# Strassen's seven products on half of K in seven FFN blocks of a two-layer fp32 trunk on Trainium2, with the weight sums made by adding DMAs

## Reference

```python
D_FF = 5632
for i in range(2):
    mod = silu(c) @ ada_w[i] + ada_b[i]        # six vectors of 2048
    ...                                        # mixer, residual, LayerNorm
    h = x * (1.0 + sc_f) + sh_f                # 256 x 2048
    y = (silu(h @ ffn_w1[i]) * (h @ ffn_w3[i])) @ ffn_w2[i]
    x = layer_norm(alpha * x + (1.0 + g_f) * y, ...)
```

## Time and profile before

| what | us |
|---|---|
| median of 3 runs (2192.49 to 2194.15) | 2193.56 |
| the profiled execution, given by its span | 2191.0 |
| PE busy in it | 2139.0 (98%) |
| DVE busy | 1596.9 (73%) |
| ACT busy | 990.1 (45%) |
| mean granted TensorE clock | 0.998 of full |
| DMA moved | 635.90 MB, mean 290 GB/s |

### The profile page before, as it was taken

The page is one execution under the profiler, slowest core; times in us unless marked ns, Lnnn a source line. Parts: engine busy times, 40 slices in busy tenths (PEclk is TensorE's granted clock), DMA queues, the critical chain, the costliest instruction groups (busy, mean ns, idle before and its releaser), DMA issues.

```text
span 2191.0 us, 24820 instructions
## 1 busy us (share of the span) xinstructions
PE 2139.0 (98%) x9557; PEld 1744.3 (80%) x9557; DVE 1596.9 (73%) x1792; ACT 990.1 (45%) x1291; POOL 105.1 (5%) x208
## 2 busy tenths in 40 slices
PE   5799999999999999999999999999999999999999
PEld 2378887888888888888788888878888888888887
DVE  6789999777777777778877666878775555455566
ACT  1077646444443444443544455554444433444443
POOL 2101100000000000000000000000000000000000
PEclk9999999999999999999999999999999999999999
DMA  9999997889998898999589788958987765666773
GB/s 387 418 364 362 363 388 285 276 292 341 337 340 319 320 340 322 318 350 361 193 287 331 264 273 282 338 175 290 332 295 226 234 194 191 214 212 213 219 239 124
DMA packets 177064, 635.90 MB, mean 290 GB/s; under 512 B 20385, under 2 KB 51377, under 8 KB 150705
## 3 DMA queue, kind: packets, MB, share of 16 engines
q1 hardware_dynamic: 147298, 427.93, 56.0%
q0 software_dynamic: 27792, 201.34, 24.6%
q10 hardware_dynamic: 1856, 5.04, 0.6%
HBM read 616.37 MB, written 17.86 MB: 289 GB/s over the span
## 4 chain that ended last, share of the span: by engine, by line
PE 86%; DMA 6%; DVE 6%; ACT 2%; issue 1%; POOL 0%; ACTq 0%; SPq 0%; DVEq 0%; POOLq 0%
PE ps L1862 53%; PE ps L1868 27%; PE ps L1879 3%; DMA gate<-in_ada_w 3%; DMA raw<-in_mla_w_o 1%; DVE wlo L1167 1%; DMA ada_head<-in_ada_w 1%; DVE ada_w L1204 1%; DVE gate L1204 1%; DMA ada_w<-in_ada_w 1%; DMA raw<-in_mla_w_uv 1%; PE ps L2091 0%; ACT whi L710 0%; DVE ada_head L1204 0%; PE ps L2121 0%
## 5 line engine op out<-in xcount | busy, mean ns | idle before, releaser
L1167 DVE TENSOR_TENSOR wlo<-raw,whi 128x1024 fp32r<-128x1024 f32 (+1 forms) x717 | 867.1, 1216 | 513.8 <-ACT whi L710 512.7
L710 ACT ACTIVATE whi<-raw 128x1024 fp32r<-128x1024 f32 (+1 forms) x717 | 756.1, 1056 | 1033.8 <-PE ps L1868 952.4
L1862 PE MATMUL ps<-whi,hT_hi 128*128 128x512 f32 x1880 | 585.7, 393 | 1.5 <-DVE hT_lo L1595 1.5
L1862 PE MATMUL ps<-whi,hT_lo 128*128 128x512 f32 x1880 | 579.5, 389 | 0.0
L1868 PE MATMUL ps<-wlo,hT_hi 128*128 128x512 f32 x1880 | 502.7, 389 | 0.0
L1862 PEld LDWEIGHTS ps<-whi,hT_lo 128*128 128x128 f32 x1880 | 352.9, 188 | 74.0
L1868 PEld LDWEIGHTS ps<-wlo,hT_hi 128*128 128x128 f32 x1880 | 352.9, 188 | 73.7
L1862 PEld LDWEIGHTS ps<-whi,hT_hi 128*128 128x128 f32 x1880 | 350.1, 188 | 72.9 <-DVE hT_lo L1595 2.0
L1204 DVE CUSTOM_DVE_ANT_0 ada_w<-ada_w,c_bc,cols 128x2048 f32<-128x2048 f32 x145 | 339.8, 2345 | 16.4 <-ACT c_bc L1050 8.4
L1862 PE MATMUL ps<-whi,uT_hi 128*128 128x512 f32 x656 | 202.0, 389 | 0.0
L1862 PE MATMUL ps<-whi,uT_lo 128*128 128x512 f32 x656 | 201.9, 389 | 0.0
(11 more groups left out here) (274 smaller groups left out, 1470.0 us busy)
## 6 DMA issues: line engine op xcount, KB each, us to landing
raw<-in_ffn_w SPq DMA_DIRECT2D x528, 512.0 KB, 4.7
ada_w<-in_ada_w POOLq DMA_DIRECT2D x145, 1024.0 KB, 7.6
raw<-in_fox_w_in SPq DMA_DIRECT2D x96, 512.0 KB, 5.3
ada_head<-in_ada_w POOLq DMA_DIRECT2D x16, 1024.0 KB, 20.3
raw<-in_mla_w_o SPq DMA_DIRECT2D x32, 512.0 KB, 8.6
raw<-in_fox_w_o SPq DMA_DIRECT2D x32, 512.0 KB, 5.5
gate<-in_ada_w POOLq DMA_DIRECT2D x12, 1024.0 KB, 9.0
ada_low<-in_ada_w POOLq DMA_DIRECT2D x10, 1024.0 KB, 10.4
```

The lines of the kernel that those rows point to most:

```text
L710: nc.scalar.activation(split_hi(pl.unit)[:, 0:n], raw[:, s, 0:n], ACT.Copy).then_inc(hi_ready, 1)
L1167: nc.vector.tensor_tensor(split_lo(pl.unit)[:, 0:n], raw[:, s, 0:n], split_hi(pl.unit)[:, 0:n].bitcast(F32), ALU.subtract).then_inc(lo_rea ...
L1862: nc.tensor.matmul(ps[:, 2 * pair + t, 0:width], a[:, t * P:(t + 1) * P], w_hi, start=(first and c == 0 and a is hi), stop=False)
```

## The change

In blocks 4 to 10 of layer 1's FFN (FAST_FROM = 4; seven blocks) the first half of K, four units deep, is done in two groups (MIXES = 2) by the Winograd form of Strassen's algorithm. The 2 x 2 blocks of the left matrix are row half t by K unit x of the group; those of the right are K unit by (w1, w3). Each of the seven products is an operand of 6 matmuls (operand), 128 rows by 512 columns into one bank. Four of them take as stationary a sum of h blocks (S1 to S4), made once on DVE while block 3 runs (mix_inputs, mix_low) and split by ACT (mix_high) into tiles that lie where c_bc and ada_w were; DVE's modulation work is therefore finished earlier (one product after every second unit in the first half of block 3, and no spare ones at the end of block 2). The weight sums T1 to T4 are not computed by an engine: POOL issues a DMA with accumulate onto the raw slot that still holds the previous operand, after its lo has been made. Their chain in a slot is B11, T1, T2, T4, and B22, T3 in another. The other half of K is done in plain units of 12 matmuls. A block has thus 22 units in the ring in place of 16, in the order of FAST_UNITS, in which group 1 follows group 0 at seven operands' distance.

Raw slots are 7 (two more lie where c_bc was, over the mixing's own input, so that loads into them wait for mix_ready), given out by raw_slots(), and a load waits for the lo of the last unit in its slot. The banks are: 0 to 3 the products of B11, T1, T2 and T3; 4 and 5 w1's plain half with B21 and T4; 6 and 7 w3's plain half with B22. DVE and ACT combine them (fast_block on each), into silu_all and u. PE waits for both pairs before each fast block, for mix_ready before the first, for each bank's reader in the fast block before, and after each pass for all of them. Units are counted from the block's start below: 0 is B11 of group 0, 21 the last plain unit.

```diff
+FAST_FROM = 4
+MIXES = 2
+FAST_GROUPS = range(MIXES)
+PLAIN_UNITS = range(2 * MIXES, PAIRS)
+FAST_BLOCKS = range(FAST_FROM, sum(FF_PASSES))
+S1, S2, S3, S4 = range(4)
+W1, W3 = "ffn_w1", "ffn_w3"
+def fast_units():
+    w1 = iter([("plain", j, W1, j, None) for j in PLAIN_UNITS])
+    w3 = iter([("plain", j, W3, j, None) for j in PLAIN_UNITS])
+    part = {"B11": (W1, 0, None), "B21": (W1, 1, None), "B22": (W3, 1, None), "T1": (W3, 0, "B11"),
+            "T3": (W3, 0, "B22"), "T2": (W3, 1, "T1"), "T4": (W1, 1, "T2")}
+    def mix(kind, g):
+        name, which, onto = part[kind]
+        return kind, g, name, 2 * g + which, onto
+    return [mix("B11", 0), mix("B21", 0), mix("B22", 0), next(w1), next(w1), mix("T1", 0), mix("T3", 0),
+            mix("B11", 1), mix("B21", 1), mix("B22", 1), next(w1), next(w1),
+            mix("T2", 0), mix("T1", 1), mix("T3", 1), next(w3), mix("T4", 0), mix("T2", 1),
+            next(w3), next(w3), mix("T4", 1), next(w3)]
...
+    for n, kind in enumerate(UNIT_KINDS):
+        if n < FAST_START:
+            s = n % RING
+        elif kind and kind[4]:
+            s = held.pop((kind[4], kind[1]))
+        else:
+            s = min((m for m in range(RAWS) if m not in held.values()), key=lambda m: last[m])
+        if kind and any(u[4] == kind[0] for u in FAST_UNITS):
+            held[kind[0], kind[1]] = s
+        slots.append(s)
+        before.append(last[s] + 1)
+        last[s] = n
...
+                if RAW_FREE[n]:
+                    sp.wait_ge(lo_ready, RAW_FREE[n])
+                if RAW_SLOT[n] >= RING:
+                    sp.wait_ge(mix_ready, 1)
+                sp.dma_start(raw_of(n)[:, 0:source.shape[-1]], source).then_inc(raw_in[RAW_SLOT[n]], 16)
...
+            def load_fast(first, i):
+                for n, (kind, g, name, j, onto) in enumerate(FAST_UNITS):
+                    if onto:
+                        pl.unit += 1
+                        continue
+                    load(A[name][1, i * PAIRS + j])
+                    if i > first and n == U_OUT_AFTER:
+                        u_out(1, i - 1)
+                    if i > first and n == U_BACK_AFTER:
+                        u_back(1, i - 1)
...
+                            pool.wait_ge(lo_ready, RAW_FREE[n])
+                            pool.dma_start(raw_of(n), A[name][1, i * PAIRS + j], accum_op=ALU.add
+                                           ).then_inc(sum_in[kind == "T3"][g], 16)
...
+            def fast_block(n, i):
+                b = i - FAST_FROM
+                units(AT["B11"] + 4)
+                act.wait_ge(units_used, pl.pe - 4)
+                act.wait_ge(u_flipped, U_BLOCKS + i)
+                nc.scalar.activation(silu_all[:, 0, :], ps[:, 0, :], ACT.Copy).then_inc(first_copied, 1)
+                units(AT["T1"] - AT["B11"] - 4)
+                act.wait_ge(units_used, pl.pe)
+                nc.scalar.activation(u[:, 1, :], ps[:, 1, :], ACT.Copy).then_inc(fifth_copied, 1)
+                units(AT["T3"] - AT["T1"])
+                if i > sum(FF_PASSES[:n]):
+                    u_high(1, n, i - 1)
+                units(AT["T4"] + 1 - AT["T3"])
+                act.wait_ge(left_done, b + 1)
+                nc.scalar.activation(silu_all[:, :, :], silu_all[:, :, :], ACT.Silu).then_inc(fast_silu, 1)
+                units(FAST_COUNT - AT["T4"] - 1)
...
+                        if l == 1 and first + i == FAST_FROM - 1:
+                            units(MIX_AT)
+                            act.wait_ge(mix_summed, 1)
+                            nc.scalar.activation(s_hi[:, :, :, :], s_32[:, :, :, :], ACT.Copy).then_inc(mix_high, 1)
+                            units(PAIRS - MIX_AT)
...
+            def mix_inputs():
+                assert pl.ada == len(ADA_ORDER), pl.ada
+                dve.wait_ge(ada_done, pl.ada)
+                chunks = 2 * UC * MIXES
+                chain(nc.vector.tensor_tensor(mix32[:, :, :], hT_hi[:, 0:chunks, :].bitcast(F32),
+                                              hT_lo[:, 0:chunks, :].bitcast(F32), ALU.add))
+                of = mix32[:, :, :].rearrange("p (g x c) (t n) -> p x t g c n", x=2, c=UC, t=T)
+                out = s_32[:, :, :, :].rearrange("p s (g c) n -> p s g c n", c=UC)
+                (a11, a21), (a12, a22) = ([of[:, x, t] for t in range(T)] for x in range(2))
+                s = [out[:, n] for n in range(4)]
+                mark(nc.vector.tensor_tensor(s[S1], a21, a22, ALU.subtract))
+                mark(nc.vector.tensor_tensor(s[S3], a11, a21, ALU.subtract))
+                own()
+                chain(nc.vector.tensor_tensor(s[S2], s[S1], a11, ALU.subtract))
+                nc.vector.tensor_tensor(s[S4], s[S2], a12, ALU.add).then_inc(mix_summed, 1)
+            def mix_low():
+                dve.wait_ge(mix_high, 1)
+                nc.vector.tensor_tensor(s_lo[:, :, :, :], s_32[:, :, :, :], s_hi[:, :, :, :].bitcast(F32),
+                                        ALU.subtract).then_inc(mix_ready, 1)
+            def fast_block(n, i):
+                b = i - FAST_FROM
+                units(AT["T3"])
+                if i > sum(FF_PASSES[:n]):
+                    u_low(1, n, i - 1)
+                units(AT["T2"] - AT["T3"])
+                dve.wait_ge(units_used, pl.pe)
+                dve.wait_ge(first_copied, b + 1)
+                chain(nc.vector.tensor_tensor(u[:, 0, :], silu_all[:, 0, :], ps[:, 2, :], ALU.add))
+                nc.vector.tensor_tensor(silu_all[:, 1, :], u[:, 0, :], ps[:, 3, :], ALU.add).then_inc(sixth_read, 1)
+                units(1)
+                dve.wait_ge(fifth_copied, b + 1)
+                dve.wait_ge(sixth_read, b + 1)
+                chain(nc.vector.tensor_tensor(u[:, 0, :], u[:, 1, :], u[:, 0, :], ALU.subtract))
+                mark(nc.vector.tensor_tensor(u[:, 1, :], u[:, 1, :], silu_all[:, 1, :], ALU.subtract))
+                units(AT["T4"] - AT["T2"] - 1)
+                dve.wait_ge(units_used, pl.pe)
+                own()
+                nc.vector.tensor_tensor(silu_all[:, :, :], silu_all[:, :, :], ps[:, 4:6, :], ALU.add
+                                        ).then_inc(left_done, 1)
+                units(FAST_COUNT - AT["T4"])
+                dve.wait_ge(units_used, pl.pe)
+                nc.vector.tensor_tensor(u[:, :, :], u[:, :, :], ps[:, 6:8, :], ALU.add).then_inc(right_read, 1)
+                dve.wait_ge(right_read, b + 1)
+                dve.wait_ge(fast_silu, b + 1)
+                chain(nc.vector.tensor_tensor(u[:, :, :], silu_all[:, :, :], u[:, :, :], ALU.mult))
+                flip(1, i, u)
...
+                        elif l == 1 and first + i == FAST_FROM - 1:
+                            units(1)
+                            mix_inputs()
+                            units(MIX_AT)
+                            mix_low()
+                            units(PAIRS - 1 - MIX_AT)
                         else:
-                            units_with_ada(PAIRS, 2)
+                            units_with_ada(PAIRS, 0 if (l, i) == (1, FAST_FROM - 2) else 2)
...
+            def operand(bank, stationary, first, end):
+                s = pl.unit % RING
+                pe.wait_ge(hi_ready, pl.unit + 1)
+                for c, (hi, lo) in enumerate(stationary):
+                    for a in (hi, lo):
+                        nc.tensor.matmul(ps[:, bank, :], a, whi[:, s, c * NB:(c + 1) * NB],
+                                         start=(first and c == 0 and a is hi), stop=False)
+                pe.wait_ge(lo_ready, pl.unit + 1)
+                for c, (hi, lo) in enumerate(stationary):
+                    ins = nc.tensor.matmul(ps[:, bank, :], hi, wlo[:, s, c * NB:(c + 1) * NB],
+                                           start=False, stop=(end and c == UC - 1))
+                ins.then_inc(units_used, 1)
+                pl.unit += 1
...
+            def fast_block(i):
+                b = i - FAST_FROM
+                pair_free(pl.block)
+                pair_free(pl.block + 1)
+                if b == 0:
+                    pe.wait_ge(mix_ready, 1)
+                for kind, j, name, _, _ in FAST_UNITS:
+                    first, end = j == 0, j == MIXES - 1
+                    if kind == "B11":
+                        if b and first:
+                            pe.wait_ge(first_copied, b)
+                        operand(0, rows_of_h(j, 0, 0), first, end)
+                    if kind == "T1":
+                        if b and first:
+                            pe.wait_ge(fifth_copied, b)
+                        operand(1, mixed(S1, j), first, end)
+                    if kind == "T2":
+                        if b and first:
+                            pe.wait_ge(sixth_read, b)
+                        operand(2, mixed(S2, j), first, end)
+                    if kind == "T3":
+                        if b and first:
+                            pe.wait_ge(sixth_read, b)
+                        operand(3, mixed(S3, j), first, end)
```

(87 more changed lines are left out.)

77 lines of the change are left out of this document (60 added, 17 removed).

## The result

The changed kernel takes 2300.26 us (2297.48 to 2301.8) against 2193.41: a ratio of 1.0484, interval 1.0469 to 1.0499, 107 us slower. The forecast was 2215 with a range of 2185 to 2248: the direction was right, the size wrong by a factor of five (107 us for 21.3). The page of the kernel after: span; busy by engine; shares of the chain by engine and by line.

What follows compares the result with a forecast made beforehand. The prediction took TensorE (PE), busy 98% of 2191.0 us, as the bound. Its terms, -19.0 + 8.0 + 3.9 + 7.7 + 5.5 + 11 + 4.2, summed to +21.3, so 2215 us, with a range of 2185 to 2248.

Steps and rivals of the forecast that it cites:

- The saving: In seven fast blocks, 84 matmuls fewer at 0.2267 us each: -19.0 us.
- the four boundaries: PE waits at the entries of blocks 4 (8.0 us) and 6 (3.9) and the exits after 5 and 10 (7.7).
- the five joints: Between fast blocks, B22 waits for banks 6 and 7, free at 3.8 but needed at 2.72: 5.5 us in all.
- The entry of block 4: First loads wait for the mixed inputs, so PE starts at 27.0 in place of 19.0: 8.0 us (bounds 3.9 and 11).
- the term of the adding DMAs: In six blocks with u's traffic, T4 of group 1 comes 1.8 us late: 11 us (bounds 0 and 35).
- L: Duration of one 512 KB adding DMA, taken as 6.5 us, between 5.4 and 7.8.
- The load of unit 11: Queued behind u's eight returns, goes at 13.4 us into the block, lands at 18.8, split just in time: no wait.
- The bound of 6.8: Load time in us behind the adding DMAs' upper bound of 35 us, with additions at 7.8.
- a rival with a chance of 0.14: DMA rings become the bound, an addition taking its engines as long as two loads: 2265 us, milder forms 2240 to 2270.
- The clock: After long PE waits the clock falls, once at block 4's entry and half a fall elsewhere: 4.2 us (0 to 11).
- Sums in time (1): Rival: adding DMAs land like loads, under 5.6 us: 2200 to 2204 us, still slower; chance 0.18.
- Faster (3): Rival: at boundaries and joints banks come free when PE asks, DVE's evictions not behind splits: 2180 us; chance 0.22.

Runs made afterwards that it cites:

- e4: The change with u's DMAs later in SP's queue and the sums' operands as independent plain SP loads, weight additions left out: 2210.77 us.
- e1: The change with u stored behind the load of unit 11 and read back behind that of unit 15 (was 9 and 10): 2271.18 us.
- e10: The change with e1's edit and POOL's DMAs copying instead of adding (weight additions left out), in the change's own order: 2236.87 us.
- e5: The change with the edits of e1 and e3, both groups in step in another order of units, u split later: 2226.86 us, ratio 1.0155.
- e3: The change with DVE reading banks before the splits ahead of them, products' banks swapped in pairs, PE waiting for a pair only where written: 2275.71 us.
- e7: The change with filler matmuls on PE, 20 before each of five joints' waits and 38 before each of two exits' waits: 2299.2 us.
- e6: The change with the edits of e3 and e4 together (weight additions left out): 2179.46 us, ratio 0.9933 to the kernel before.
- e11: e5 with one group in place of two, and the mixing's input moved off the two added raw slots: 2186.04 us, ratio 0.9966.

## Why the prediction was wrong

**Right.** The saving (84 matmuls), PE as the bound before, the four boundaries and the five joints as places of new waits. e4, where only they are left, shows their sum within 1 us of the forecast: 26.1 us for 25.1 (10.0 + 8.0 + 4.4 + 3.7). The entry of block 4 was 2.0 low, the joints 1.1 high in all.

**The step that failed** is the term of the adding DMAs, 11 us with bounds of 0 and 35, measured at 60 (e1 less e4), and at 89 with the load behind u's returns (the change less e4). Taken away one after the other, the loss of 107 us is 29 for the place of u's DMAs (change to e1), 34 for the adding (e1 to e10), 26 for the chain of DMAs and POOL's queue (e10 to e4) and 17 for the boundaries less the saving (e4 to before); in another order the parts differ. Four things in the term:

1. "Whatever the duration L, T4 is ready at 26.6 + 2L, so the wait begins at L = 5.6." This asked when PE needs the sum. But T4's split is in DVE's program ahead of the reads that free six of the eight banks (2 and 3 by L1845 and L1846, 4 and 5 by L1855, 6 and 7 by L1859; ACT reads 0 and 1). Once its lead is short, each microsecond lost moves those reads, before PE waits for the sum. e10 shows it: with copies PE waits 0.3 us for a sum, and joints, exits and the entry still take 18.5 us more. By an estimate on the forecast's own clock, DVE needs 9.5 us from T4's split to the left-half addition and 1.2 for that, and PE gets from T4 to B21 in 5.4, so T4 had to be ready 5.3 us before PE wants it, at 32.5 in place of 37.8; with 26.6 + 2L that is L = 3.0, less than even the quiet load's 3.9. In the change T4 came only when PE asked, so the joints took 4.6 us each in place of 1.1, for the left half that the forecast had at 0 with 0.3 to spare, and the exits 8.7 in place of 3.9.
2. The load of unit 11 was to go 13.4 us into the block and land 5.4 later, "just in time", as in the stage at 330 GB/s. In block 7 it went at 19.4 and took 9.0, with adding DMAs on the same rings: u was stored at 10.9, where the forecast had it flipped at 6.4, late because the joint itself waits 4.65 us, and the eight returns took 5.4 to issue for 3.75. So the late read feeds the late load, and that the next sums. The bound of 6.8 was no bound. e1 prices it at 29 us; the place was right, the size was not.
3. L was taken as 6.5; the median is 7.9 (7.1 in the added slots), at the upper bound of 7.8. In the forecast's own formula this gives 4.6 us in place of 1.8 in six blocks, 28 for 11: the size of L alone is the smaller part of the miss.
4. What an addition does to the others was left to a rival with a chance of 0.14. It holds the rings 2.8 to 3.0 us, twice a load. In the change's own order the rings still had gaps (0.86 in a block), so this came in as latency; in e5 it is the bound itself. That rival's price, 2240 to 2270, was low for the change (2300), and it had the joints at 1.1 too; e5, where the rings are the bound and e3's edits have taken most of the boundaries, is under it at 2227.

**The clock** was given 4.2 us. Matmuls took 39 us longer in the change, but e7 shows that this is no term of its own there: taking away some 23 us at the lower level bought nothing, since the chain sets the pace. In e4, where no chain does, PE is busy 8.4 us longer for it, twice the forecast and inside its 0 to 11.

**The rivals.** Sums in time (1) had 2200 to 2204; e4 without any chain has 2211, by the entry and the clock above, and e10, whose chain of copies lands near that rival's 5.6, has 2237, by the step that failed. Faster (3) needed DVE's reads ahead of their splits: e3 and e6 made that, and e6's 2179 is where that rival put it (2180), but only with no chain. The change itself leaves the splits first, as the forecast said against this rival.

## What to carry to other kernels

When a change adds a dependent DMA, test its lateness at every engine that has it in program order, not only at its consumer: in e10 a copy that reached PE in time had already pushed back the reads that freed PE's banks. Price a new kind of transfer by its ring time as well as its latency, sum both over the stage, and take only as many as the rings have room for: here a quarter of K paid (e11), half of it didn't (e5). And where a wait is filled with work and the time stays, look for the chain, not for the idle engine.
